# Twelve query and key tiles of the first projection as three products of split parts, in a kernel of three transformer layers on one core

## What is computed

```
def hybrid_layer(x, mem, g_mix, w_in, ...):
    hn = rms_norm(x, g_mix)
    proj = hn @ w_in
    q_d, k_d, v_d, q_b, k_b, v_b, q_m = jnp.split(proj, cuts, axis=-1)
    q_d = rms_norm(split_heads(q_d, N_HEADS_DIL), qg_dil)
    ...
    kv = rms_norm(mem, g_memtok) @ w_mem_kv
    ...
    x = x + peer_ffn(rms_norm(x, g_ffn), w_peer_q, sub1, sub2, peer_u, peer_v)
```

## Time and profile before

| | us |
|---|---|
| median of 3 runs | 2116.81 |
| lowest and highest of them | 2115.47, 2116.89 |
| the profiled execution, its own time | 2118.32 |
| span of its profile | 2116.5 |
| PE busy in it | 2032.2 (96%) |
| DVE busy | 1512.6 (71%) |
| ACT busy | 1080.7 (51%) |
| POOL busy | 210.1 (10%) |

### The profile page before, as it was taken

How to read it: one execution, slowest core, us unless ns; L and a number is a source line. 1 busy time by engine, 2 the same in 40 slices (tenths; PEclk the granted TensorE clock), 3 DMA queues, 4 the chain that set the end, 5 groups by cost and what they waited for, 6 DMA issues and landing times.

```text
span 2116.5 us, 44708 instructions
## 1 busy us (share of the span) xinstructions
PE 2032.2 (96%) x15166; PEld 1910.4 (90%) x15166; DVE 1512.6 (71%) x3542; ACT 1080.7 (51%) x2217; POOL 210.1 (10%) x218
## 2 busy tenths in 40 slices
PE   8998999878999999999999999999999999999998
PEld 6757889867999999999989888999998978899998
DVE  4755499598667888888876367877666647777666
ACT  3241266697444444444446455654445655655444
POOL 0000199683000000000000000000000000000000
PEclk9999999999999999999999999999999999999999
DMA  7333555402558777787644543445554553355553
GB/s 291 130 130 111 227 170 169 139 0 71 183 184 291 280 279 272 277 279 276 233 154 165 178 146 110 133 160 185 179 182 137 180 179 111 100 167 172 183 184 109
DMA packets 103533, 375.96 MB, mean 178 GB/s; under 512 B 11504, under 2 KB 11776, under 8 KB 103168
## 3 DMA queue, kind: packets, MB, share of 16 engines
q1 hardware_dynamic: 89280, 323.86, 45.6%
q10 hardware_dynamic: 14144, 50.72, 6.2%
HBM read 373.47 MB, written 1.05 MB: 177 GB/s over the span
## 4 chain that ended last, share of the span: by engine, by line
PE 81%; DVE 8%; issue 5%; POOL 3%; DVEq 2%; ACT 2%; DMA 0%; ACTq 0%; POOLq 0%
PE bank L750 21%; PE bank L756 21%; PE bank L753 21%; PE bank L562 5%; POOL part_lo L1518 3%; DVE one_hots L1783 2%; PE bank L701 1%; PE bank L943 1%; PE bank L899 1%; PE bank L981 1%; DVE part_lo L1938 1%; PE bank L863 1%; PE bank L869 1%; PE bank L842 1%; PE bank L866 1%
## 5 line engine op out<-in xcount | busy, mean ns | idle before, releaser
L1188 ACT ACTIVATE part_hi<-ring 128x512 fp32r<-128x512 f32 x1080 | 664.2, 626 | 419.2 <-PE bank L753 395.3
L1799 DVE TENSOR_TENSOR part_lo<-ring,part_hi 128x512 fp32r<-128x512 f32 x684 | 453.2, 689 | 215.5 <-ACT part_hi L1188 210.2
L750 PE MATMUL bank<-u_hi,part_hi 128*128 128x256 f32 (+1 forms) x1792 | 516.8, 288 | 21.5 <-POOL part_lo L1518 10.2
L756 PE MATMUL bank<-u_hi,part_lo 128*128 128x256 f32 (+1 forms) x1792 | 504.0, 281 | 0.0
L753 PE MATMUL bank<-u_lo,part_hi 128*128 128x256 f32 (+1 forms) x1792 | 502.3, 280 | 0.0
L750 PE MATMUL bank<-w_hi,part_hi 128*128 128x256 f32 x1376 | 389.4, 283 | 3.5 <-DVE w_lo L1828 2.1
L753 PE MATMUL bank<-w_lo,part_hi 128*128 128x256 f32 x1376 | 388.6, 282 | 0.0
L756 PE MATMUL bank<-w_hi,part_lo 128*128 128x256 f32 x1376 | 388.6, 282 | 0.0
L750 PEld LDWEIGHTS bank<-u_hi,part_hi 128*128 128x128 f32 (+1 forms) x1792 | 336.3, 188 | 31.8 <-POOL part_lo L1518 12.2
L756 PEld LDWEIGHTS bank<-u_hi,part_lo 128*128 128x128 f32 (+1 forms) x1792 | 338.8, 189 | 0.5
L753 PEld LDWEIGHTS bank<-u_lo,part_hi 128*128 128x128 f32 (+1 forms) x1792 | 336.9, 188 | 1.3
(11 more groups left out here) (278 smaller groups left out, 2982.3 us busy)
## 6 DMA issues: line engine op xcount, KB each, us to landing
ring<-stream_dram SPq DMA_DIRECT2D x606, 512.0 KB, 3.3
arena<-ada_dram ACTq DMA_DIRECT2D x96, 512.0 KB, 4.7
xT<-x_dram SPq DMA_DIRECT2D x4, 256.0 KB, 5.5
arena<-mem_dram SPq DMA_DIRECT2D x1, 1024.0 KB, 10.0
arena<-keys_dram SPq DMA_DIRECT2D x1, 1024.0 KB, 5.3
out_dram<-uT SPq DMA_DIRECT2D x4, 256.0 KB, 2.4
cst<-consts_dram SPq DMA_DIRECT2D x1, 841.0 KB, 15.1
cond<-cond_dram SPq DMA_DIRECT2D x1, 512.0 KB, 15.9
```

Source lines behind the costliest of these rows:

```text
L750: m = pe.matmul(o, hi, u(cc), start=first, stop=False, **flags)
L756: m = pe.matmul(o, lo, u(cc), start=False, stop=last, **flags)
L1188: act.activation(part_hi[:, h % 4, 0:width], ring[:, n % RING, (h % 2) * width:(h % 2 + 1) * width], ACT.Copy).then_inc(hi_ready, 1)
L1799: v.tensor_tensor(part_lo[:, h % 4, :], ring[:, n % RING, (h % 2) * 512:(h % 2 + 1) * 512], part_hi[:, h % 4, :], ALU.subtract).then_inc(l ...
```

## The change

Tiles 2 to 13 go through `passes` in place of `linear`. The parts of their weights are 24 halves that use the same four buffers and counters as the expert stage (all later counts are raised by 24): ACT makes the high parts, two per tile, in its own list around the evictions; POOL makes the low parts. The normed input gets a high part `x_hi` (ACT, eight copies) and a low part `x_lo` (DVE, eight subtractions behind the normed chunks). These two lie where the slabs of `ada_early` go, so `fetch_early(0)` moves from behind tile 2 to behind tile 13 on ACT. The sums of the memory's squares, its root and the Silu move from behind tile 1 to behind tile 2. On ACT the squares of the memory now stand behind four high parts and `x_hi`. Before the expert stage ACT now makes three high parts ahead and the fourth behind the evictions of the key products. `passes` and `split_half` themselves are the same and only stand earlier in the file.

```
@@ PE
             for j in range(W_IN_QK + MEM_K):
-                if j < W_IN_QK:
+                if j < QK_PLAIN:
                     linear(S_QK + j, T_QK + j, uT, DC, fresh=(x_normed, 0) if j == 0 else None)
+                elif j < W_IN_QK:
+                    b = free_bank(T_QK + j)
+                    for h in (2 * (j - QK_PLAIN), 2 * (j - QK_PLAIN) + 1):
+                        m = passes(h, 0, lambda c: (b[:, 0:S], c == 0, c == DC - 1),
+                                   lambda c: x_hi[:, c, :], lambda c: x_lo[:, c, :],
+                                   (xlo_chunk, 0) if j == QK_PLAIN else None)
+                    m.then_inc(tile_full, 1)
                 else:
                     linear(S_QK + j, T_QK + j, memT, DC)
-                if j == 1:
+                if j == 2:
                     pe.wait_ge(mem_sq, 1)
@@ ACT, behind the root of the input and before the squares of the memory
+            def first_high(h):
+                split_half(S_QK + QK_PLAIN + h // 2, h, 0, 0)
+
+            for h in range(4):
+                first_high(h)
+            for c in range(DC):
+                act.wait_ge(x_normed, c + 1)
+                act.activation(x_hi[:, c, :], uT[:, c, :], ACT.Copy).then_inc(xhi_chunk, 1)
@@ ACT, the loop over tiles
             for j in range(W_IN_QK + MEM_K):
+                if 2 <= j < W_IN_QK - 2:
+                    first_high(2 * j)
                 evict(T_QK + j, qk[:, j, :])
-                if j == 1:
+                if 2 <= j < W_IN_QK - 2:
+                    first_high(2 * j + 1)
+                if j == 2:
                     act.wait_ge(mem_sum, 1)
...
-                if j == 2:
+                if j == W_IN_QK - 1:
                     fetch_early(0)
                 if j >= 3 and j % 2:
                     pair_root((j - 3) // 2)
@@ ACT, before the expert stage
             high_parts(0, 0)
-            high_parts(1, 0)
+            split_half(S_PEER + 1, 2, 0, QUERY_END)
             for j in range(8):
                 evict(T_KEYS + j, ...)
+            split_half(S_PEER + 1, 3, 0, QUERY_END)
@@ POOL
+            for h in range(QK_HALVES):
+                low_half(S_QK + QK_PLAIN + h // 2, h, 0)
@@ DVE
             for c in range(DC):
                 normed(uT[:, c, :], xT[:, c, :], vec[:, V_GMIX + c:V_GMIX + c + 1], rstd[:, 0:S], x_normed)
+            for c in range(DC):
+                v.wait_ge(xhi_chunk, c + 1)
+                v.tensor_tensor(x_lo[:, c, :], uT[:, c, :], x_hi[:, c, :], ALU.subtract).then_inc(xlo_chunk, 1)
```

More of the change, by code:

```diff
@@ L70 @@
     int(x) for x in np.cumsum([0, 2 * L_UQ, 48, 24, 16, 6 * FT]))
-assert all(h % 4 == 0 for h in (PEER_HALVES, LH_GATE, LH_WO, LH_OUT, LH_FFN, L_HALVES))
+assert all(h % 4 == 0 for h in (QK_HALVES, PEER_HALVES, LH_GATE, LH_WO, LH_OUT, LH_FFN, L_HALVES))
 def slot_of_half(h):
@@ L591, in pair_sum, with passes @@
                 pe.matmul(bank[6 + p % 2][:, :], BONES, pairsq[:, p, :], start=True, stop=True).then_inc(psum_ready, 1)
+            def passes(h, before, outs, u, l, fresh=None, width=P, bank_done=None, **flags):
+                pe.wait_ge(lo_ready, before + (h + 1))
+                for c in range(4):
+                    cc = (h % 2) * 4 + c
+                    hi = part_hi[:, h % 4, c * width:(c + 1) * width]
+                    lo = part_lo[:, h % 4, c * width:(c + 1) * width]
+                    o, first, last = outs(cc)
+                    if fresh is not None:
+                        pe.wait_ge(fresh[0], fresh[1] + (cc + 1))
+                    m = pe.matmul(o, hi, u(cc), start=first, stop=False, **flags)
+                    if c == 0 and h % 2 == 0:
+                        m.then_inc(slot_begun, 1)
+                    m = pe.matmul(o, hi, l(cc), start=False, stop=False, **flags)
+                    if c == 0:
+                        m.then_inc(half_begun, 1)
+                    m = pe.matmul(o, lo, u(cc), start=False, stop=last, **flags)
+                    if bank_done is not None and cc in (1, 3, 5):
+                        m.then_inc(bank_done, 1)
+                return m
             pe.wait_ge(ones_loaded, 16)
@@ L737, in _ @@
                 m.then_inc(tile_full, 1)
[L739 to L759, removed]
             def expert_act(i, k, turns, slots=12):
@@ L1085, in _, with split_half, split_slot, high_parts @@
             root_of(root[:, 0:S], bank[2][:, 0:S]).then_inc(x_root, 1)
+            def split_half(n, h, uses, before, width=512):
+                act.wait_ge(loaded[n % RING], (uses + (n // RING + 1)) * 16)
+                if not isinstance(before, int) or before + h >= 4:
+                    act.wait_ge(half_begun, before + (h - 2))
+                act.activation(part_hi[:, h % 4, 0:width], ring[:, n % RING, (h % 2) * width:(h % 2 + 1) * width],
+                               ACT.Copy).then_inc(hi_ready, 1)
+            def split_slot(n, k, uses, before):
+                for h in (2 * k, 2 * k + 1):
+                    split_half(n, h, uses, before)
+            def high_parts(k, turns, slots=12):
+                split_slot(S_PEER + k, k, turns * (slots // RING), turns * (2 * slots) + QUERY_END)
+            def first_high(h):
[5 more added lines that the diff above has]
+                act.activation(x_hi[:, c, :], uT[:, c, :], ACT.Copy).then_inc(xhi_chunk, 1)
             act.wait_ge(mem_loaded, 16)
@@ L1181, in gelu @@
                     .then_inc(gelu_done, 1)
[L1183 to L1187, removed]
-                act.activation(part_hi[:, h % 4, 0:width], ring[:, n % RING, (h % 2) * width:(h % 2 + 1) * width],
-                               ACT.Copy).then_inc(hi_ready, 1)
-            def split_slot(n, k, uses, before):
-                for h in (2 * k, 2 * k + 1):
-                    split_half(n, h, uses, before)
-            def high_parts(k, turns, slots=12):
-                split_slot(S_PEER + k, k, turns * (slots // RING), turns * (2 * slots))
             high_parts(0, 0)
-            high_parts(1, 0)
+            split_half(S_PEER + 1, 2, 0, QUERY_END)
             for j in range(8):
```

26 lines of the change are left out of this document (17 added, 9 removed).

## The result

The changed kernel takes 2124.43 us (median of five; 2123.34 to 2129.24) where the kernel before takes 2116.81 (2111.17 to 2117.01). The ratio is 1.0038, with a 95% interval of 1.0028 to 1.0049, so it is slower, by 0.4%. A second set of five, beside which the kernel before had 2116.80, gave 2122.91 us and 1.0043 (1.0026 to 1.006). The forecast was 2118.7 with no change as the likeliest sign, in a range from 2110.5 to 2124.0. The time is just outside it, and the mechanism is that of the second rival, to which 0.20 was given: GpSimd gets in between any two of VectorE's two-input instructions.

The account below looks back on a forecast made before the run. PE was taken to bound the first stage at 7.77 us per pair, DVE close at 6.0. Moved fetch 0.6, clock 1.0 and expert stage 0.3 sum to +1.9 us, median 2118.7, range 2110.5 to 2124.

Parts of the forecast that it names:

- the second rival: First stage: POOL gets in between any two of DVE's two-input instructions; pair 8.4 us, total 2121.3; chance 0.20.
- What bounds the kernel, and the saving on PE: First stage: PE sets the pace, DVE close behind; three products save 0.63 us per tile, 7.6 us for twelve.
- Two DVE instructions issued back to back without a drain are not parted: First stage: POOL must wait for a whole run of DVE instructions; a pair then takes 7.3 us.
- Normed input: Start of the stage: the run of eight normed chunks keeps POOL out, so nothing moves up to 25.3 us.
- Memory: DVE's run from 34.9 to 40.7 us: memory chunks 3.25, bias tables 0.95, squares and tables 1.6, POOL kept out.
- Pairs: Pairs of tiles behind tile 5: four low parts plus 2.5 us of excluding DVE instructions, 7.3 us against 7.77 before.
- The clock: PE's idle time before tile 5 brings a stretch at 1.2 GHz, costing 1.0 us, between 0 and 1.7.
- The moved fetch: ACT, behind tile 13: eight issues delay pair 5's root, so the gain is gone and the head comes 0.6 us later.
- The memory's root behind tile 2: ACT: the memory's root is ready at 33.0 us where it was at 29.26.
- the first rival: First stage: SCALAR_TENSOR_TENSOR does not contend with POOL, first head 5.7 us earlier, total 2111.4; chance 0.22.
- the third rival: First stage: the long reciprocal shuts POOL out; pair 10.65 us, +13.4 us, total 2132; chance 0.10.
- The expert stage: Start of the expert stage: the fourth high part comes late and PE waits 0.3 us, between 0 and 1.3.

Follow-up runs that it names:

- no_read: Changed kernel with POOL's 24 first-stage subtractions replaced by zero fills that read nothing, low weight parts left out; 2111.86 us, ratio 0.998.
- one_input_pool: Changed kernel with POOL's 24 first-stage subtractions replaced by multiplications by zero, reading one tensor instead of two; 2118.89 us (one run).
- before_fetch_late: Kernel before the change with only the fetch of the first modulation slabs moved to where the change puts it; 2118.59 us, ratio 1.0009.
- memory_early: Changed kernel with the memory's sums, root and Silu back behind tile 1, as before the change; 2119.89 us, ratio 1.0024.

## Why the prediction was wrong, step by step

**What bounds the kernel, and the saving on PE: right.** With DVE undisturbed (no_read) the change brings 5.1 us, and root to head is 72.06 us against 77.1 and 77.4. But "DVE is not far behind" was the warning: 6.0 of 7.77 us left 1.8 us of room per pair, and two waits of 1.1 us are more.

**The step that failed: "Two DVE instructions issued back to back without a drain are not parted".** It came from one place with a one-input instruction on POOL's side, and I carried it over to subtractions with two inputs; one_input_pool shows that it doesn't hold in general for one input either. The profile of the changed kernel shows the reverse in three pairs: 1.66 and 1.65 us for two tables back to back in the first of them. Four terms hang on it.

- Normed input. I had the run of eight keep POOL out, so "up to 25.3 us nothing moves". It took 7.31 us. Tiles 0 and 1 end at 29.4, 4.1 us late: 1.0 is the later start, and the rest is the parted run and a longer stretch at half clock (10.2 against 6.9 us) together. Profiles with none of that clock at the start part the two. ACT takes tile 1 from PSUM at 24.65 in the second profile of the changed kernel, whose reciprocal came at 12.27, and at 21.97 in before_fetch_late, whose came at 12.31:

```profile
24.65 0.38 ACT L1083 ACTIVATE arena<-bank 128x256 f32<-128x256 f32 x1 [1.08 <-PE bank L570]
```

```profile
21.97 0.38 ACT L1068 ACTIVATE arena<-bank 128x256 f32<-128x256 f32 x1 [3.07 <-PE bank L562]
```

  That is 12.4 us from the reciprocal against 9.7, so the parted run costs 2.7 us before tile 1, twice the second rival's 1.3.
- Memory. From the start of the run to the reciprocal of pair 0's root I had 5.8 us (34.9 to 40.7); it took 10.9 (38.89 to 49.76), of which 4.15 and 1.06 are waits for POOL. Neither the forecast nor the rival had this, and it is the largest single miss.
- Pairs. I had 7.3 us, the rival 8.4; measured 8.16, 8.22 and 8.13 at 54.15, 62.31, 70.53 and 78.66. The rival's sum was right in kind; its term for one wait is 1.10 us and not 1.2.
- PE's idle time. I expected 3.8 us before tile 5, released by POOL. PE's timeline has it, 3.78 us, but in front of a pair's sum and released by DVE's squares:

```profile
48.95 1.12 PE L599 MATMUL bank<-arena,cst 128*128 128x512 f32 x2 [3.78 <-DVE arena L1606]
```

The size fits by chance; the cause is another. The second profile has the same 3.78 us in the same place.

**The clock: seen, but free.** The granted clock did fall behind that idle time (busy times by stretch, changed kernel):

```profile
15.90:26.10 10.20, 9.17 (x18) 5.51 (x19) 9.70 (x16) 7.15 (x20) 5.55 (x4) 0.50 0.57 226
...
50.00:53.40 3.40, 3.40 (x18) 3.40 (x17) 3.30 (x2) 0.84 (x2) 1.28 (x1) 0.50 0.49 157
```

From 50.0 to 53.4 PE ran at 1.2 GHz, as long as I had said. I charged 1.0 us for it. DVE, which was on the path, waited for nothing from 37.06 on, so it cost nothing. The first row is the start of the stage, where the lower clock does count; the profile before had 6.9 us of it there and five others none. The second profile of the changed kernel had none there either, with the same kind of parted run, so that run alone doesn't bring it.

**The moved fetch: mechanism right, price wrong.** In the changed kernel the issues are where I put them:

```profile
78.78 4.29 ACTq L1135 DMA_DIRECT2D arena<-ada_dram  x8
```

They end at 83.07. The root behind them waited until 83.64 for DVE to release the buffer, so DVE's delay hides them with half a microsecond to spare. Where DVE isn't late the wait shows, 2.77 us in no_read, 3.49 in before_fetch_late, and even then it cost 0.3 us at the head in the latter. "The gain is gone" was wrong as a reason; the gain went to the subtractions.

**The memory's root behind tile 2.** I had it 7.7 us behind tile 1 (33.0 against 25.3), and it came 7.6 behind (37.03 against 29.4). The step is right, but I costed it at nothing for DVE, and in memory_early the median is 3.0 us lower.

**Kinds of instruction.** SCALAR_TENSOR_TENSOR contends as TENSOR_TENSOR does: taken right, and the first rival falls. The size of one wait was read loosely, though: I took about 2.3 us for 2048 elements "by the 0.69 us for 512", and four times 0.69 is 2.76. The 1.10 us above replaces it. The reciprocal leaves POOL alone: right, from a thin row, and the third rival falls.

**The expert stage: wrong sign.** I added 0.3 us. The last eviction ahead of it is 3.03 us later than before (257.59 against 254.56) and the first Gelu 2.63 (271.06 against 268.43). With three high parts ahead in place of four, ACT's first evictions of key products begin 2.51 us later, not 3.03 (259.43 against 256.92): the shorter list ahead of them gives 0.5 us, and POOL's part a half later takes only a little of it.

**The sum.** The first head is 6.34 us late, but the spans of the two profiles differ by 4.7 us only. The stretches at half clock fit that: the kernel before had one from 144 to 154 us in its profiled execution and the changed kernel none there, while the changed kernel had two that the other lacked, 422 to 425.5 us and some 3.4 us more behind 1115. That they make the whole difference is not shown. Over many executions, 6.1 and 7.6 us stand against the second rival's 4.5; what it lacked is above all the memory's run with 4.15 us, the 3.0 us of its late root, and the other half of the parted run at the start, of which not all reaches the end.

## To carry to other kernels

Before work is given to GpSimd, count on VectorE's side the two-input instructions that fall beside it and not the free time: each of GpSimd's two-input subtractions cost VectorE 1.0 to 1.1 us wherever such an instruction followed, back to back or not (15 of 24 did), and VectorE had 1.8 us of room per pair. If it must be done, put VectorE's two-input work where GpSimd has nothing ready, and its one-input reciprocals beside it; twelve tables moved that way gave 3.4 to 4.9 us, about half of it by filling VectorE's idle time, and all such moves together turned a loss of 0.4% into a gain of 0.1 to 0.25%. And a rule read from one place in a trace holds for the kinds of instruction in that place.

## What was not expected of the hardware

- GpSimd and VectorE alternate instruction by instruction inside a run of VectorE instructions with no drain between them: eight chunks of 0.41 us with four subtractions beside them took 7.31 us in place of 3.26.
- How long VectorE waited went with how many tensors the GpSimd instruction reads, with one operation tried of each kind: 1.10 us for a subtraction of 128x512 that takes 1.28, 0.42 for a one-input instruction of the same size that takes 1.49, nothing for one that only writes (0.53).
- Eight DMA issues on ScalarE's queue, feared as a cost of 3 to 5 us, were a gain where they held back the high parts that would have set GpSimd going.
- The kernel's time varies by 3 to 11 us within a set of executions, and stretches at half clock lie in other places each time: 6.9 and 10.2 us of them at the start of two profiles, and none before the first head in five others.
